# Two stacked transformer blocks in float32: transposes of the second block's attention moved into the projections, and a wait of the rotary angles moved to its first use

## The reference

```
for l in range(2):
    h = h + hybrid_mixer(rmsnorm(h, attn_norm[l]), ...)       # 6 MLA, 6 differential, 4 MoBA heads, then @ w_out
    n = rmsnorm(h, cross_norm[l])
    q = n @ wq;  k, v = split(rmsnorm(mem, mem_norm[l]) @ wkv) # 4 heads of 256, memory of 256 rows
    h = h + softmax(q k^T / 16) v @ wo
    h = h + square(relu(rmsnorm(h, mlp_norm[l]) @ w1)) @ w2
out = rmsnorm(h, final_norm)
```

## Time and profile before

| | |
|---|---|
| median of 3 runs | 2614.95 us (2604.96 to 2618.14) |
| profiled execution | 2604.36 us, span 2602.6 us |
| granted TensorE clock, mean | 0.949 of full |
| PE busy | 2493.5 us (96%) |
| DVE busy | 1811.1 us (70%) |
| ACT busy | 1478.2 us (57%) |
| DMA | 565 MB, 217 GB/s over the span |

### The profile page before, as it was taken

One profiled execution on the slowest core, in us unless ns is written; L12 is line 12 of the kernel. 1 busy time (PEld: TensorE's weight loads), 2 busy tenths in 40 slices (PEclk: granted clock), 3 DMA queues, 4 the chain that ended last, 5 costly groups with the idle time before them and its releaser, 6 DMA issues.

```text
span 2602.6 us, 31787 instructions
## 1 busy us (share of the span) xinstructions
PE 2493.5 (96%) x11894; PEld 2090.7 (80%) x11894; DVE 1811.1 (70%) x2378; ACT 1478.2 (57%) x1807; POOL 48.6 (2%) x70
## 2 busy tenths in 40 slices
PE   7899999989899999999999999997989999898998
PEld 5787888878788888888888888786878888787887
DVE  5766445675688888888898888866546556654655
ACT  5334444633477777777777777656444445554442
POOL 0000000000000000000000000000000000000000
PEclk9859999975899999999999999998999999899999
DMA  7303555420299999999999999740635553163551
GB/s 227 130 1 132 191 192 179 132 97 1 103 361 348 367 349 369 348 371 344 368 347 370 342 378 340 289 169 26 243 104 178 192 167 111 71 221 111 181 184 51
DMA packets 250693, 565.24 MB, mean 217 GB/s; under 512 B 8993, under 2 KB 23777, under 8 KB 250593
## 3 DMA queue, kind: packets, MB, share of 16 engines
q1 hardware_dynamic: 250592, 563.90, 61.2%
HBM read 562.82 MB, written 1.05 MB: 217 GB/s over the span
## 4 chain that ended last, share of the span: by engine, by line
PE 83%; issue 8%; DVE 6%; ACT 3%; POOL 1%; DMA 0%; DVEq 0%; POOLq 0%; ACTq 0%
PE PS L795 23%; PE PS L797 23%; PE PS L796 23%; PE PS L931 3%; PE PS L962 3%; PE PS L943 2%; PE PS L1089 1%; ACT SM L1385 1%; PE PS L1123 1%; PE PS L1097 1%; DVE Wl L1704 1%; DVE scr L1849 1%; PE PS L874 1%; PE PS L1016 1%; PE PS L854 0%
## 5 line engine op out<-in xcount | busy, mean ns | idle before, releaser
L2077 DVE TENSOR_TENSOR Wl<-ring,Wh 128x2048 fp32r<-128x2048 f32 x334 | 760.2, 2292 | 104.6 <-ACT Wh L1495 104.5
L1495 ACT ACTIVATE Wh<-ring 128x2048 fp32r<-128x2048 f32 x334 | 639.4, 1917 | 130.4 <-PE PS L797 130.2
L1704 DVE TENSOR_TENSOR Wl<-ring,Wh 128x2048 fp32r<-128x2048 f32 (+3 forms) x194 | 435.7, 2252 | 332.1 <-ACT Wh L1314 331.7
L1314 ACT ACTIVATE Wh<-ring 128x2048 fp32r<-128x2048 f32 (+3 forms) x194 | 365.4, 1892 | 267.3 <-PE PS L797 267.3
L795 PE MATMUL PS<-Wh,HTh 128*128 128x512 f32 (+3 forms) x1184 | 465.2, 393 | 23.2 <-DVE Wl L1704 14.0
L797 PE MATMUL PS<-Wh,HTl 128*128 128x512 f32 (+3 forms) x1184 | 458.9, 388 | 0.0
L796 PE MATMUL PS<-Wl,HTh 128*128 128x512 f32 (+3 forms) x1184 | 458.4, 387 | 0.0
L795 PE MATMUL PS<-Wh,xgh 128*128 128x512 f32 x896 | 353.5, 395 | 2.5 <-DVE xgl L1711 2.5
L797 PE MATMUL PS<-Wh,xgl 128*128 128x512 f32 x896 | 349.5, 390 | 0.0
L796 PE MATMUL PS<-Wl,xgh 128*128 128x512 f32 x896 | 348.8, 389 | 0.0
L795 PEld LDWEIGHTS PS<-Wh,HTh 128*128 128x128 f32 x1184 | 225.1, 190 | 68.2 <-issue 9.5
(11 more groups left out here) (283 smaller groups left out, 2778.6 us busy)
## 6 DMA issues: line engine op xcount, KB each, us to landing
ring<-in_moe_w_gate SPq DMA_DIRECT2D x112, 1024.0 KB, 7.1
ring<-in_moe_w_up SPq DMA_DIRECT2D x112, 1024.0 KB, 7.2
ring<-in_moe_w_down SPq DMA_DIRECT2D x112, 1024.0 KB, 6.8
ring<-in_mlp_w SPq DMA_DIRECT2D x64, 1024.0 KB, 5.1
ring<-in_w_in SPq DMA_DIRECT2D x28, 1024.0 KB, 6.0
ring<-in_w_out SPq DMA_DIRECT2D x16, 1024.0 KB, 5.2
ring<-in_cross_wkv SPq DMA_DIRECT2D x16, 1024.0 KB, 10.8
ring<-in_ffn_w_gate SPq DMA_DIRECT2D x14, 1024.0 KB, 5.1
```

Source lines behind the costliest of these rows:

```text
L1314: act.activation(Wh[:, i % SPLITS, 0:n], ring[:, r % RING, 0:n], ACT.Copy).then_inc(w_hi, 1)
L1495: act.activation(Wh[:, (base + i) % SPLITS, :], ring[:, (raw + i) % RING, :], ACT.Copy).then_inc(e_hi, 1)
L1704: dve.tensor_tensor(Wl[:, i % SPLITS, 0:n], ring[:, r % RING, 0:n], Wh[:, i % SPLITS, 0:n].bitcast(F32), ALU.subtract).then_inc(w_lo, 1)
L2077: dve.tensor_tensor(Wl[:, (base + i) % SPLITS, :], ring[:, (raw + i) % RING, :], Wh[:, (base + i) % SPLITS, :].bitcast(F32), ALU.subtract) ...
```

## The change

Mixer, w_out: the four batches of turned output are taken in the order 3, 2, 0, 1 (a batch is 256 columns; 3 and 2 hold MoBA and differential heads, ready after unit 7). Batches 3 and 2 are turned behind probs(11), before values(10); batch 0 behind values(11), when unit 9 is stored; batch 1 inside the w_out projection behind tile 0. This projection runs half 1 before half 0 (its two pieces are loaded in that order) and waits per pair of chunks. DVE makes the low parts of the first two batches before the end of unit 11. The mixer's split of a w_out piece moves from i = 4 to i = 0 (ACT, ahead of `take_block(4)`) and i = 1 (DVE).

Cross attention: the keys are turned in the third and fourth key/value projections, the first half of the queries inside the last query projection, whose `mid` is now `begin` (scores of units 0 and 1). The second half of the queries is turned as extras of unit 0. The output is turned in two parts as above, in the order 0, 1, 2, 3.

First block: DVE waits for the sine and the exponential only after its next norm statistics. All products and sums stay, but one projection per layer adds its chunks in another order.

```diff
-                for half in range(2):
+                for half in halves:                               # loads; w_out n=0: (1, 0), n=1: (0, 1)
+        MIX_ORDER = (3, 2, 0, 1)
+        cross_extras = {0: t_cross_q[2:4]}
@@ tensor
+            def mixed_linear(order, u_end):
+                first = c.turn - 3
+                def ready(pair, step, t):
+                    if step == 0:
+                        pe.wait_ge(o_out, u_end - 1 + t)
+                    pe.wait_ge(turn_out, first + order.index(pair) + 1)
+                linear(512, halves=(order[0] // 2, order[2] // 2), ready=ready,
+                       after_tile=lambda: turn_after(u_end, [t_mix2[order[3]]]))
@@ attention.finish
                             probs(i - 1)
+                        if i == n and tail:
+                            tail[1](u0 + tail[0])
@@ second block, tensor
                 finish()
-                rows()
-                turn(t_mix2)
-                pe.wait_ge(turn_out, c.turn)
-                linear(512)
+                turn_after(c.unit - 2, t_mixed[2:3])
+                mixed_linear(MIX_ORDER, c.unit)
...
-                linear(512, mid=lambda: (added(x0), turn_half(X, 0)))
+                linear(512, mid=lambda: (added(x0 + 4), turn(t_cross_k[0:2])))
+                linear(512, after_tile=lambda: turn(t_cross_k[2:4]),
+                       mid=lambda: (added(x0), pe.wait_ge(turn_out, c.turn), turn_half(X, 0)))
                 linear(512, after_tile=lambda: turn_half(X, 1))
-                linear(512)
-                pe.wait_ge(lin_out, c.lin)
-                turn(t_cross)
-                for step in attention(cross_units()):
-                    step()
-                turn(t_mix2)
-                pe.wait_ge(turn_out, c.turn)
-                linear(512)
+                q0 = c.lin
+                begin, finish = attention(cross_units(), cross_extras, (2, lambda n: turn_after(n, t_mix2[0:2])))
+                linear(512, after_tile=lambda: (added(q0), turn(t_cross_q[0:2])), mid=begin)
+                finish()
+                turn_after(c.unit, t_mix2[2:3])
+                mixed_linear((0, 1, 2, 3), c.unit)
@@ scalar
-                          {0: lambda: take_block(4), 4: another})
+                          {0: lambda: (another(), take_block(4))})
...
+                another()
+                turn(t_cross_q[0:2])
+                attention(cross_units(), cross_extras, {0: lambda: (another(), take_query(1))})
@@ vector
-                dve.wait_ge(trig_ok, 1)            # end of angles()
...
                 mean_eps(24, HD, lambda: convolve(10))
+                if layer == 0:
+                    dve.wait_ge(trig_ok, 1)
+                    lambdas_done()                 # memset, wait for lam_ok, five small operations
...
-                    if i == 4:
+                    if i == 1:
                         c.piece += 1
                         ahead()
+                    elif i == n - 1:
+                        turn_mix(t_mixed_lo[0:2], t_mixed[0:2])
```

More of the change, by code:

```diff
@@ L694, in _ @@
                 for n in range(2):
[L695 removed]
+                    lin_block(a["w_out_2"][layer], n * 512, 512, (1 - n, n))
                 sp.wait_ge(o_full, 24 + c.unit + 12)
@@ L803, in lin_bank, with linear @@
                 return 4 + (c.lin - 1) % 4
-            def linear(n, late=None, mid=None, after_tile=None):
+            def linear(n, late=None, mid=None, after_tile=None, halves=(0, 1), ready=None):
                 banks = [lin_bank() for _ in range(T)]
-                for half in range(2):
-                    if half == 1 and late:
+                for step, half in enumerate(halves):
+                    if step == 1 and late:
                         late()
@@ L815, in linear @@
                             kc = half * HALF + i
+                            if ready and i % 2 == 0:
+                                ready(kc // 2, step, t)
                             mm = product(PS[:, banks[t], 0:n], HTh[:, kc, tok(t)], HTl[:, kc, tok(t)], w,
-                                         (slice(None), i), kc == 0, kc == KC - 1)
-                        if half == 1:
+                                         (slice(None), i), (step, i) == (0, 0), (step, i) == (1, HALF - 1))
+                        if step == 1:
                             mm.then_inc(lin_full, 1)
-                        if (half, t) == (0, 0) and after_tile:
+                        if (step, t) == (0, 0) and after_tile:
                             after_tile()
-                    if half == 0:
+                    if step == 0:
                         mm.then_inc(w_half, 1)
@@ L908, in rows, with attention @@
                 pe.wait_ge(rows_ready, c.misc)
-            def attention(units, extras={}):
-                turns = c.turn
+            def attention(units, extras={}, tail=None):
                 u0, n = c.unit, len(units)
@@ L919, in scores @@
                     if i < 2:
-                        pe.wait_ge(turn_out, turns)
+                        pe.wait_ge(turn_out, c.turn)
                     if un["needs"]:
@@ L1270, in _, with mixed @@
                 turn(t_diff)
-                begin, finish = attention(diff_units(layer) + moba_units() + mla_units(), mix_extras)
+                def mixed(n):
+                    rows()
+                    turn_after(n, t_mixed[0:2])
+                begin, finish = attention(diff_units(layer) + moba_units() + mla_units(), mix_extras, (8, mixed))
                 linear(IN2_BLOCKS[4][1], mid=begin)
@@ L1653, in _ @@
                             row_scale()
-                    else:
-                        c.piece += 1
-                        ahead()
+                        elif n == 2:
+                            turn(t_cross_k[0:2])
+                    else:
+                        another()
+                        turn(t_cross_k[2:4])
                         norm(col2(layer, "cross", 8), BY_HALF[0:2])
@@ L1662, in _, with take_query @@
                 norm(col2(layer, "cross", 8), BY_HALF[2:4])
[L1663 to L1667, removed]
+                def take_query(n):
                     for t in range(T):
                         take(CQ[:, t, n * 512:n * 512 + 512], scale=row_rs[:, 0, t:t + 1])
-                turn(t_cross)
-                attention(cross_units())
+                c.piece += 2
+                ahead()
+                row_scale()
+                take_query(0)
+                another()
+                turn(t_cross_q[0:2])
+                attention(cross_units(), cross_extras, {0: lambda: (another(), take_query(1))})
                 turn_mix(t_mix2)
@@ L2397, in _, with between_cross @@
                 norm(col2(layer, "cross", 8), BY_HALF[2:4])
-                c.piece += 4
+                c.piece += 3
                 ahead()
-                attention(cross_units())
+                def between_cross(i, n):
+                    if i == 1:
+                        c.piece += 1
+                        ahead()
+                    elif i == n - 1:
+                        turn_mix(t_mix2_lo[0:2], t_mix2[0:2])
+                c.turn += len(t_cross_k) + 2
+                attention(cross_units(), cross_extras, between_cross)
                 c.lin += 12
-                c.turn += len(t_cross)
-                turn_mix(t_mix2_lo, t_mix2)
+                turn_mix(t_mix2_lo[2:4], t_mix2[2:4])
                 add_out(col2(layer, "mlp", 8))
```

24 lines of the change are left out of this document (16 added, 8 removed).

## The result

| | before | after |
|---|---|---|
| median | 2611.52 us (9 runs, 2602.3 to 2618.1) | 2596.6 us (9 runs, 2591.8 to 2601.4) |
| ratio, 95% interval | | 0.9949 (0.9934 to 0.9964) |
| profiled execution, span | 2602.6 us | 2594.4 us |
| mean granted clock, that execution | 0.949 | 0.944 |

The account below looks back on a forecast made before the run. PE, busy 96% of the span, was taken to bound the kernel through its standing and low clock. Terms of -9.2, -10.2, -6.4 and -4.4 summed to -30.2 us; forecast 2584 us, range 2568 to 2601.

Parts of the forecast that it names:

- Angles: First block's start: PE's 7.1 us wait before the fourth projection goes, 2.7 of clock gained, 0.6 charged; -9.2 us.
- The clock term of 2.7: First block's start: 2.7 us lost to a granted clock of 0.50 behind the 7.06 us wait would be regained.
- Cross attention: Second block's cross attention: moved turns and scores shorten PE's waits, -2.2 us per layer, -4.4 in all.
- Turned output: Mixer's end: the w_out product starts sooner, -2.4 us per layer, and 1.6 of clock in the first; -6.4 us.
- The split: Both mixers, unit 5: standing -4.6 and -2.3 us, clock -3.5 and -1.0, 1.2 charged; -10.2 us.
- PE's row for exponentials: Sign for right, second block: the 6.3 us wait goes and the row falls from 15.2 to some 6.
- the wait for `Wl` at the start: Sign for right, first block: PE's wait for DVE's low parts of weights shrinks from 12.2 to about 5 us.
- The sign for "wrong": An equal wait under another name in the same stretch, or granted clocks of 0.5 staying between mixer units 3 and 7.
- (a): Whole kernel: only the standing goes, the clock doesn't come back; 17.8 us gained, 2597 us; chance 0.20.
- (b): Mixers and cross attention: waits move behind ACT's high parts and copies; 10.6 us left, 2604 us, same; chance 0.12.
- (c): Cross attention's projections become bound by the weight splits; slower, 2635 us; chance 0.03.
- (d): First block: DVE's freed split waits for its high part instead of the sine, reducing the gain; no chance of its own.

Follow-up runs that it names:

- b_keep_mix: Kernel before with three useless, overwritten matmuls ahead of the scores of units 2 to 11 in both mixers; 2607.9 us, ratio 0.9985.
- n_keep_mix: Kernel after with the mixer's split put back at i = 4 and three useless matmuls ahead of scores of units 2 to 11; 2588.6 us, ratio 0.9911.
- e_split: Kernel before with only the mixer's split of a w_out piece moved from i = 4 to i = 0 and 1; 2616.9 us, ratio 1.0031.
- a_nosplit: Kernel after with the mixer's split of a w_out piece put back at i = 4; 2583.6 us, ratio 0.9901.
- a_keep_mix: Kernel after with three useless, overwritten matmuls ahead of the scores of units 2 to 11 in both mixers; 2576.95 us, ratio 0.9882.
- e_angles: Kernel before with only the angles' part of the change, DVE's two waits moved; 2596.5 us, ratio 0.9959.
- a_idle: Kernel after with 14 useless DVE products at i = 4 of both mixers, where the kernel before stood for its split; 2589.2 us, ratio 0.9925.

## Why the prediction was wrong

The time lies inside the range, but the gain, 13 to 15 us, is less than half of the 30 forecast.

**Angles: right.** -9.2 forecast; the fifth projection came 9.74 us sooner and kc_sb 9.06 (118.10 to 109.04), so 0.7 came back where 0.6 was charged. The clock term of 2.7 was real. Not all of it arrives in each execution: the three profiled kernels with the old waits begin the first mixer at 1753.2 to 1754.9 us, the ten with the new ones (and no filling in the first block) at 1742.6 to 1748.4, and the kernel after, at 1747.95, is only 6.7 us ahead there.

**Cross attention: right.** -2.2 per layer forecast, -2.6 measured. The waits are those listed: 0.8; 0.6 and 0.7 where I had 1.7; 0.7; 1.25 where I had 1.4.

**Turned output: right in kind, somewhat larger with filling.** -2.4 per layer and 1.6 of clock in one: from b_keep_mix to n_keep_mix unit 5 to w_out is 3.3 us shorter (less 0.5 of turns in the product), and the mixer 4.5 and 4.4, since the product's start no longer runs at half clock in either layer. That is 8.9 us against 6.4. In the kernel after, the first product still begins at 0.50, so there the 1.6 wasn't seen.

**The split: here it failed.** The forecast was -10.2 us: "With the split gone ... -4.6 us" and "between 0 and 5; I take 3.5". The standing went as worked out: 6.29 to 1.67 us in the first mixer. The clock term had the wrong sign, and so had its bound ("a busy stretch at half clock costs at most half of itself, so between 0 and 5"): it looked only at the low stretch that was there and never asked whether a new one could come. With filling the move is worth 5.1 us per mixer. Left alone it costs: e_split is 8 us slower than before, and the kernel after 12.5 slower than a_nosplit. In the profiled executions the time at half clock up to w_out went from 16 and 17 us to 35 and 27. It had been around the stand (units 5 to 6); now most of it is in units 7 to 11, where PE is busy throughout and the others wait for it, up to the start of the w_out product in the first mixer.

Of the signs that the prediction named, PE's row for exponentials fell to 9.2 and not to some 6; the others for "right" came as written (the wait for `Wl` at the start fell from 12.2 to 5.4). The sign for "wrong" looked for low clocks between units 3 and 7; they came mostly behind.

**The rivals.** (a) gave 2597 and the measurement is 2596.6, but its mechanism isn't the one shown: it let all clock terms be zero, while that of the angles was real, that of the product's start came with filling, and that of the mixer was a loss. Its number is right by luck. (b), waits that move, is refuted: no wait of the size came, and b_keep_mix less a_keep_mix is 31 us (27 by the ratios). That this is so near 30.2 is partly luck too. Without clock terms the forecast had 10.5 us for the two mixers; between these runs they give 19.2, because with filling the second mixer has the full stand as well, and because b_keep_mix still has some 10 us at half clock per mixer, the start of the product included, that a_keep_mix hasn't. (c) did not occur. (d) did not either: DVE's low parts began at 47.62 us without a pause, and the whole stand went. The Trainium skill's sentence on the clock (TensorE: Matmul & The Clock Gate, "What's actually happening"), that activity lifts the default low clock at a point that varies, agrees with the filling runs and, so far as it goes, with the difference between two mixers of the same code in one execution (80.0 and 85.2 us in e_angles). It doesn't account for a low clock that persists while the rows show PE fully busy; that stands here by the measurement.

Taking 2602.6 us and one profile as the base misled too: that execution was one with short low stretches. The kernel before ranges over 16 us (2602.3 to 2618.1); with filling in the mixers its runs lie within 5, so most of the range is probably the clock there.

Left open: why the clock falls in units 7 to 11, and why a stand of 6 us at unit 5 keeps it away. a_idle shows only that it did in the two mixers of its trace (the stretch from unit 5 to w_out took 29.7 and 29.5 us there, 39.1 and 34.8 in the kernel after).

## What to carry to other kernels

Before counting a removed stall as time, ask at which clock PE will run the work behind it: in stretches of small matmuls the clock may pay the stall back with interest. Hold the clock with a few overwritten matmuls in such a stretch, in both kernels, and compare: the runs become narrow and each step shows its price. Read the granted clock of both all the same: here it still fell for some 7 us behind a stand of 5.49 us. Where PE is busy at 1.2 GHz and the other engines wait for it, this filling is a gain in itself (here from 0.9949 to 0.9797 of the kernel before, some 40 us).

## What the runs showed of the hardware

PE can show 100% busy and stay at a granted clock of 0.50 for 40 us and more: 151 instructions in 40 us in the first block's attention, against 240 (204 without the filling) at 0.98. A useless 0.23 us matmul per attention unit was enough to take nearly all late low stretches out of the mixers; in the first block's attention three per unit, behind 14 in the pause before it, were too few; with six a stretch of 40 us ran at 0.98 in the first layer and one at 0.94 (560 to 600 us) in the second. Removing a stall made the kernel 8 us slower, and 8.25 us of useless DVE work per layer did not make it slower at all.
